# The experts' weights stored tile by tile in memory, one run of 8 KB a partition

## The reference, cut to what matters

```
D_MODEL, N_EXPERTS, TOP_K, D_EXP = 1024, 8, 2, 3584

def moe_swiglu(h2, w_router, w_gate, w_up, w_down):
    top_logits, top_idx = lax.top_k(h2 @ w_router, TOP_K)
    top_w = jax.nn.softmax(top_logits, axis=-1)
    ...                                   # each token goes to two of eight experts
    hid = silu(ragged_dot(xs, w_gate, sizes)) * ragged_dot(xs, w_up, sizes)
    y = ragged_dot(hid, w_down, sizes)
    ...                                   # y * top_w, added back to the token's row
```

## Time and profile before

| what | value |
|---|---|
| median of three runs | 3207.98 us |
| the profiled execution, its own time | 3211.1 us |
| its span | 3209.3 us |
| PE busy | 3073.3 us (96%) |
| DVE busy | 2302.4 us (72%) |
| ACT busy | 1750.2 us (55%) |
| mean granted TensorE clock | 0.984 |
| experts' stage, from 2197 to 3192 us of the span | 995 us |

### The profile page before, as it was taken

The page is one execution under the profiler, slowest core; times in us unless marked ns, Lnnn a source line. Parts: engine busy times, 40 slices in busy tenths (PEclk is TensorE's granted clock), DMA queues, the critical chain, the costliest instruction groups (busy, mean ns, idle before and its releaser), DMA issues.

```text
span 3209.3 us, 37966 instructions
## 1 busy us (share of the span) xinstructions
PE 3073.3 (96%) x15010; PEld 2523.9 (79%) x15010; DVE 2302.4 (72%) x2125; ACT 1750.2 (55%) x1641; POOL 46.1 (1%) x28
## 2 busy tenths in 40 slices
PE   8999999999999899998998999988999999999998
PEld 6777887877888788777886877777888888887886
DVE  7886556886655655766446576757888888888888
ACT  4564445465444345453333454535777777776765
POOL 0000000100000000000000000000000000000000
PEclk9999999999999999999999999998999999999999
DMA  6434555443565554335555543338999999999997
GB/s 245 144 120 144 190 183 181 148 132 120 186 190 170 177 168 161 119 119 171 193 162 170 181 161 112 125 106 283 356 361 341 357 359 343 360 348 341 368 338 262
DMA packets 351087, 697.24 MB, mean 217 GB/s; under 512 B 12224, under 2 KB 17216, under 8 KB 350784
## 3 DMA queue, kind: packets, MB, share of 16 engines
q1 hardware_dynamic: 347024, 687.75, 62.7%
q10 hardware_dynamic: 3888, 7.07, 0.7%
HBM read 693.73 MB, written 1.05 MB: 216 GB/s over the span
## 4 chain that ended last, share of the span: by engine, by line
PE 76%; DVE 10%; DMA 4%; ACT 4%; DVEq 3%; issue 2%; PEld 0%; ACTq 0%; POOL 0%; PEldq 0%
PE banks L642 22%; PE banks L644 22%; PE banks L643 22%; DVE weights_low L1594 4%; ACT weights_high L1196 2%; DMA weights_raw<-in_moe_w_up_dram 2%; PE banks L797 1%; DMA weights_raw<-in_moe_w_down_dram 1%; PE banks L679 1%; PE banks L1107 1%; DMA weights_raw<-in_moe_w_gate_dram 1%; PE banks L754 1%; ACT weights_transposed L1375 1%; PE banks L783 1%; PE banks L1045 1%
## 5 line engine op out<-in xcount | busy, mean ns | idle before, releaser
L1594 DVE TENSOR_TENSOR weights_low<-weights_raw,weights_high 128x2048 fp32r<-128x2048 f32 (+1 forms) x658 | 1490.2, 2269 | 491.4 <-ACT weights_high L1196 485.0
L1196 ACT ACTIVATE weights_high<-weights_raw 128x2048 fp32r<-128x2048 f32 (+1 forms) x658 | 1247.9, 1899 | 548.7 <-PE banks L644 434.4
L642 PE MATMUL banks<-weights_high,h_transposed_high 128*128 128x512 f32 x2784 | 1107.9, 398 | 21.2 <-DVE weights_low L1594 9.7
L644 PE MATMUL banks<-weights_high,h_transposed_low 128*128 128x512 f32 x2784 | 1084.9, 390 | 0.0
L643 PE MATMUL banks<-weights_low,h_transposed_high 128*128 128x512 f32 x2784 | 1083.9, 389 | 0.0
L642 PEld LDWEIGHTS banks<-weights_high,h_transposed_high 128*128 128x128 f32 x2784 | 526.5, 189 | 147.4 <-DVE weights_low L1594 15.8
L644 PEld LDWEIGHTS banks<-weights_high,h_transposed_low 128*128 128x128 f32 x2784 | 525.8, 189 | 110.4
L643 PEld LDWEIGHTS banks<-weights_low,h_transposed_high 128*128 128x128 f32 x2784 | 527.2, 189 | 102.0 <-issue 1.0
L642 PE MATMUL banks<-weights_high,y_transposed_high 128*128 128x512 f32 x1096 | 433.5, 396 | 6.6 <-DVE y_transposed_low L1711 2.8
L644 PE MATMUL banks<-weights_high,y_transposed_low 128*128 128x512 f32 x1096 | 427.1, 390 | 0.0
L643 PE MATMUL banks<-weights_low,y_transposed_high 128*128 128x512 f32 x1096 | 427.0, 390 | 0.0
(11 more groups left out here) (311 smaller groups left out, 2063.7 us busy)
## 6 DMA issues: line engine op xcount, KB each, us to landing
weights_raw<-in_w_in_dram SPq DMA_DIRECT2D x152, 1024.0 KB, 5.0
weights_raw<-in_moe_w_gate_dram SPq DMA_DIRECT2D x114, 1024.0 KB, 7.0
weights_raw<-in_moe_w_up_dram SPq DMA_DIRECT2D x112, 1024.0 KB, 6.3
weights_raw<-in_moe_w_down_dram SPq DMA_DIRECT2D x112, 1024.0 KB, 6.7
weights_raw<-in_w_up_dram SPq DMA_DIRECT2D x32, 1024.0 KB, 5.5
weights_raw<-in_w_down_dram SPq DMA_DIRECT2D x32, 1024.0 KB, 5.0
weights_raw<-in_ffn_w_gate_dram SPq DMA_DIRECT2D x10, 1024.0 KB, 5.1
weights_raw<-in_ffn_w_up_dram SPq DMA_DIRECT2D x10, 1024.0 KB, 5.1
```

Source lines behind the costliest of these rows:

```text
L642: nc.tensor.matmul(out_of[t], lhs(0, k, t), high[:, k], start=begin, stop=False)
L644: mm = nc.tensor.matmul(out_of[t], lhs(1, k, t), high[:, k], start=False, stop=end)
L1196: nc.scalar.activation(tile_view(WH, h % SPLIT, tile), tile_view(raw, h % RAW, tile), ACT.Copy).then_inc(high_ready, 1)
L1594: v.tensor_tensor(tile_view(WL, h % SPLIT, tile), tile_view(raw, h % RAW, tile), tile_view(WH, h % SPLIT, tile).bitcast(F32), ALU.subtract ...
```

## The change

The host lays the three expert matrices out anew before the launch, so that a tile is one block of memory of 1 MB, and inside it each partition's 4 x 512 numbers are one run of 8 KB. The load of a tile in the experts' stage then copies 128 x 2048 numbers, one run a partition, into the whole buffer. All other weights stay row by row and go through line 603 as before. No instruction is added, removed or moved on any engine.

```
+def tile_by_tile(w):
+
+    n, e, rows, cols = w.shape
+    return (w.reshape(n, e, rows // (KT * P), KT, P, cols // NB, NB).transpose(0, 1, 2, 5, 4, 3, 6)
+            .reshape(n, e, rows // (KT * P), cols // NB, P, TILE))
...
                     def load(h, expert, done=0):
 
                         tile = st["tiles"][h % EXPERT]
-                        src = a[tile["name"]][tile["layer"], bass.ds(expert, 1), tile["row"]:tile["row"] + tile["rows"] * P,
-                                              tile["col"]:tile["col"] + tile["width"]].rearrange("e (k p) c -> p (e k) c", p=P)
+                        src = a[tile["name"]][tile["layer"], bass.ds(expert, 1), tile["row"] // (KT * P),
+                                              tile["col"] // NB].rearrange("e p c -> p (e c)")
                         sp.wait_ge(low_ready, STATIC + h - RAW + 1 + done)
-                        sp.dma_start(tile_view(raw, (STATIC + h) % RAW, tile), src).then_inc(landed[(STATIC + h) % RAW], 16)
+                        sp.dma_start(raw[:, (STATIC + h) % RAW], src).then_inc(landed[(STATIC + h) % RAW], 16)
...
+    for name in ("moe_w_gate_2", "moe_w_up_2", "moe_w_down_2"):
+        laid[name] = tile_by_tile(np.asarray(inputs[name]))
```

## The result

The changed kernel takes 3214.57 us, the median of 22 runs (3210.26 to 3220.76), beside 3209.62 us for the kernel before in 22 runs. The ratio is 1.0015, with a 95% interval from 1.0009 to 1.0021. Run again later on another chip, beside the kernel before (3205.68 us), it took 3215.04 us, ratio 1.0028 [1.0016, 1.0041]. So the forecast of 3199 us, 0.28% faster, had the wrong sign: the change costs 0.15 to 0.28%, and 3214.57 lies just beyond the end of the range, 3214.

The account below looks back on a forecast made before the run. The prediction took PE, stopped by late loads in the experts' stage, as the bound: of 10.7 us of load-caused stops 9 come back, other terms zero, so from the median 3208.0 to 3199 us, range 3190 to 3214.

Parts of the forecast that it names:

- What bounds the kernel: Experts' stage: PE and DMA engines both nearly full; late loads stop PE, costing 10.7 us of 14.6 us of stops.
- The 8 stops once an expert: Experts' stage: PE stops with DVE's extra steps for the choice of tokens, not loads; 3.9 us that stay.
- no room: Experts' loads: just fast enough, 2.95 us of all 16 engines a tile beside PE's 2.99 us.
- The run in memory: Experts' loads: 8 KB runs for 2 KB win 0.21 us a tile, 2.95 to 2.74 us; DMA share to 0.92.
- what comes and goes: Experts' loads: 0.24 us a tile between a full stretch at 384 GB/s and the mean of 349, taken as unchanged.
- What of that reaches PE: Experts' stage: at 2.74 us a tile nearly all load-caused PE stops go, 9 of 10.7 us.
- A: Experts' loads: memory, not packets, holds them at 349 GB/s; 3208 us, DMA share stays 0.98; chance 0.22.
- B: Experts' loads: runs starting 8 KB apart make the 16 engines collide; 3225 to 3291 us; chance 0.12.
- C: Experts' stage: all 16.3 us of PE stops go, also those put down to DVE's extra steps; 3192 us; chance 0.11.
- The issue on SP: Experts' loads: up to 0.16 us more to issue each, hidden in SP's waits for DVE; counted as nothing.

Follow-up runs that it names:

- e1: Kernel before, experts' loads bringing only the first 128 of each 512 columns (results wrong), against the kernel before: 3196.74 us, ratio 0.9965.
- e6 to e8: Two more raw buffers in the experts' stage, with rows, 8 KB runs and 4 KB runs, against the kernel before: ratios 0.9976, 0.9975, 0.9979.
- e3: 8 KB runs, each starting 14,336 bytes after the last, against the kernel before: 3217.78 us, ratio 1.0027.
- e11: 8 KB runs, each starting 8,704 bytes after the last (512 unused), against the kernel before: 3210.93 us, ratio 1.0018.
- e2: Tiles as 1 MB blocks, row group behind row group, runs still 2 KB, against the kernel before: 3218.96 us, ratio 1.0033.
- e5: A partition's four 2 KB runs side by side, 512 bytes unused behind each, against the kernel before: 3214.23 us, ratio 1.0025.
- e12: A partition's two 4 KB runs side by side, 512 bytes unused behind each, against the kernel before: 3219.93 us, ratio 1.0048.

## Why the prediction was wrong, point by point

**What bounds the kernel: right in the main.** PE with stops, and loads that come late. That late loads cost 10.7 us was confirmed in size: 10.9 us of the stage's length go when there are none (e1, e6 to e8), ratio 0.9965 and 0.9975 to 0.9979, which is 12.0 and 7.0 to 7.5 us by the medians. The 8 stops once an expert stay, as forecast. But the prediction's "no room" was too strict: without the overlap of the records the engines need 2.83 us a tile and not 2.95, under PE's 2.99.

**The run in memory: right in sign, far too large, 0.03 us for 0.21.** The packets fell to 217,232, about the 217,000 expected. The prediction took the 0.24 us between the tiles at the program's start and the constants as the price of short runs. But the 2.71 us of those tiles hold stalls: free of them 2 KB packets take 2.56 us a tile, so the runs alone are worth 0.11 and not 0.21. And it left what comes and goes as it was, while the stalls grew by 0.08 us a load. The share fell to 0.94, near the 0.92 of the forecast, but three quarters of that fall come from the overlap of the records: with a quarter of the packets there is less of it.

**What of that reaches PE: this is the step that failed.** It said that with loads at 2.74 us of engine time the reserve does not shrink, and so that ACT's waits fall under 30 us and 9 us come back. It took the mean of 16 engines for the time of a load. A load lands with its last engine, and in the stage the last one is 1.2 us behind the middle one before and 1.5 us after. The middle engine gave 0.2 us, and the last one took them back (6.56 us before, 6.65 and 6.58 after). ACT's waits for loads rose from 99.5 to 108.7 and 111.8 us, the long ones among them most, PE's stops did not become fewer, and the time rose. That nothing was won follows from this; why 5 to 9 us were lost, when the mean landing is so nearly the same, is shown only as far as ACT's longer waits.

**The rivals.** A, the loads stay where they are, is nearest in time, 3208 us, and the engines' work did stay nearly where it was, 2.80 us a tile for 2.83; the share of 0.98 that it expected fell, for the most part by the counting. That the memory is what holds the loads, as A says, no run shows. B, the new addresses collide, had the right sign and a price far too high (3225 to 3291 us for 3214.57), and what I held against it was weak: I compared rows 14,336 and 4,096 bytes apart, and neither has a partition's runs side by side. Placing does cost, up to 0.5%, and nothing for 4 KB runs in halves; taking the step off the power of two did not bring the time back (e3, e11). C did not come in any run: even with a deeper ring, which takes every late load away, the 8 stops once an expert stay, at 3198 us and not 3192.

The Trainium skill, "DMA: Bandwidth & Descriptors", section "Latency and other measured facts", names tiles laid out in one piece as a remedy for rows that lie a large power of two apart. By its table a step of 512 KB gave 207 GB/s where the full rate was 214; the prediction called that the full rate, and it is nearly so. The rows here lay 14,336 and 4,096 bytes apart, and laying the tiles out in one piece cost 0.33% (e2) at packets of 2 KB. The same page's 512 B for line rate (section "Specifications") does not quite fit an engine's own time here, 80 ns from start to start for 2 KB and 306 for 8 KB, 4% less a byte; for the kernel's time it came out right that 2 KB was enough.

**The issue on SP** got shorter and not longer, 0.33 us for 0.37, so the 0.16 us more that the constants suggested did not come; where it did come, in e5 and e12, the prediction's fear that it would eat the gain can't be ruled out:

```profile
2640.50 0.33 SPq L619 DMA_DIRECT2D weights_raw<-in_moe_w_up_dram  x1
```

**Open:** why the stalls at the start of a load grew, and what made ACT's single waits longer. It is not simply how evenly the engines finish: in the mean the first and the last engine are 1.6 us apart before and 1.9 us after, but only 1.5 us in e12, the slowest kernel. The traces show where and how much, not what in the memory does it.

## What to carry to other kernels

A load is as late as its slowest DMA engine. A falling DMA share says nothing on landings, and with longer packets it falls in part only because fewer records overlap; look at the longest waits of the loads' consumer, and at the landings (here the mean landing did not rank the kernels). Where the queue is near full and a few late loads stop the bound engine, a deeper ring of buffers buys the loss back (here 0.21 to 0.25%, with buffers that were idle in that stage), in all three layouts that were tried, and then long runs add nothing. When weights are laid out anew for longer runs, try more than one order: in this kernel 4 KB runs in halves were level with rows and 8 KB runs were not. Look at SP's issue time too: an order can change it.

## What the runs showed of the hardware that I had not expected

- A packet of 2, 4, 8 and 12.9 KB is recorded as 84, 159, 309 and 502 ns long in the median, and for the first three an engine starts the next one 80, 155 and 306 ns after it: 25.6, 26.4 and 26.8 bytes a ns for one engine. From 4 KB on little is left to gain.
- In a queue that is never empty for long, the 16 engines finish one load 1.6 us apart in the mean (before), 1.9 us (after); for the weight loads earlier in the program, where the engines are half idle, 0.56 us.
- The stalls sit at a load's start: its first 8 KB on an engine take some 120 ns more than usual as four packets and some 207 ns more as one; 43% of the first packets that could be followed in the changed kernel took over 1.3 times the usual time.
- How long SP takes to issue a load of 1 MB depends on its shape and order in memory: 0.33 us for one run of 8 KB a partition, 0.37 for rows or runs that lie far apart, 0.54 for several runs of one partition side by side with gaps (e5, e12).
